# RWKV state stage: k^T V moved into TensorE's first wait, and fewer products of unused result around it

## The reference, cut to what matters

```python
def step(state, inp):
    rt, wt, kt, vt, kkt, at = inp
    sa = jnp.einsum('bhvk,bhk->bhv', state, -kkt)
    state = (state * wt[:, :, None, :]
             + sa[..., :, None] * (kkt * at)[..., None, :]
             + vt[..., :, None] * kt[..., None, :])
    yt = jnp.einsum('bhvk,bhk->bhv', state, rt)
    return state, yt
...
_, y = lax.scan(step, s0, xs)
```

## Time and profile before

| what | value |
|---|---|
| median of 3 runs | 4917.19 us (4914.18 to 4917.27) |
| profiled execution, its own time | 4909.85 us |
| its span | 4908.1 us |
| granted PE clock over the span | 0.947 of full speed |
| stage `rwkv`, PE's first to last product | about 1844 to 2551 us of the span |
| PE busy in the span | 4321.2 us (88%) |
| DVE busy in the span | 2583.5 us (53%) |

### The profile page before, as it was taken

One profiled execution on the slowest core, in us unless ns is written; L12 is line 12 of the kernel. 1 busy time (PEld: TensorE's weight loads), 2 busy tenths in 40 slices (PEclk: granted clock), 3 DMA queues, 4 the chain that ended last, 5 costly groups with the idle time before them and its releaser, 6 DMA issues. The chain is left out here.

```text
span 4908.1 us, 68587 instructions
## 1 busy us (share of the span) xinstructions
PE 4321.2 (88%) x25175; PEld 3600.6 (73%) x25232; DVE 2583.5 (53%) x5011; ACT 1320.3 (27%) x2626; POOL 598.3 (12%) x585
## 2 busy tenths in 40 slices
PE   8999688888599968999978996999989799799879
PEld 6777577777477757888867885778767677577657
DVE  4444434433466656777753334778733433577733
ACT  3223211111222211111112113666621211222211
POOL 0000011111100002333330110000000011011100
PEclk9999799999799988999988998999989899899989
DMA  3111311111433331111113234310033422422233
GB/s 134 48 60 60 126 49 56 63 58 50 151 131 131 131 118 48 36 45 45 45 39 135 109 116 145 104 35 18 10 129 116 155 103 88 154 87 91 75 130 117
DMA packets 218307, 434.14 MB, mean 88 GB/s; under 512 B 36419, under 2 KB 90436, under 8 KB 218022
## 3 DMA queue, kind: packets, MB, share of 16 engines
q1 hardware_dynamic: 218150, 432.08, 25.7%
HBM read 248.40 MB, written 146.93 MB: 81 GB/s over the span
## 5 line engine op out<-in xcount | busy, mean ns | idle before, releaser
L235 PE MATMUL rp_pj<-rp_w_high,rp_hT_high 128*128 128x512 f32 (+1 forms) x640 | 239.3, 383 | 27.2 <-DVE rp_w_low L178 14.4
L235 PE MATMUL fp_pj<-fp_w_high,fp_hT_high 128*128 128x512 f32 (+2 forms) x640 | 220.7, 359 | 46.1 <-DVE fp_w_low L178 46.1
L2515 DVE TENSOR_SCALAR_CACHE_REDUCE fa_sm<-fa_sc 128x512 f32<-128x512 f32 (+2 forms) x320 | 194.4, 610 | 91.9 <-PE fa_sc L2356 80.4
L236 PE MATMUL rp_pj<-rp_w_low,rp_hT_high 128*128 128x512 f32 (+1 forms) x640 | 233.5, 374 | 0.0
L235 PE MATMUL hg_pj<-hg_w_high,hg_hT_high 128*128 128x512 f32 x512 | 210.4, 411 | 16.1 <-DVE hg_w_low L178 16.1
L235 PE MATMUL rc_pj<-rc_w_high,rc_hT_high 128*128 128x512 f32 (+1 forms) x512 | 191.8, 382 | 36.2 <-DVE rc_w_low L178 36.0
L236 PE MATMUL fp_pj<-fp_w_low,fp_hT_high 128*128 128x512 f32 (+2 forms) x640 | 219.1, 357 | 0.0
L236 PE MATMUL hg_pj<-hg_w_low,hg_hT_high 128*128 128x512 f32 x512 | 205.6, 402 | 0.0
L2370 PE MATMUL fa_tp<-fa_ident,fa_sm 128*128 128x128 f32 x1088 | 176.0, 283 | 30.5 <-DVE fa_pT_low L178 14.8
L2463 ACT CAST fa_pT_high<-fa_tp 128x512 fp32r<-128x512 f32 (+1 forms) x288 | 160.9, 559 | 148.9 <-PE fa_tp L2370 146.7
L178 DVE TENSOR_TENSOR fa_pT_low<-fa_tp,fa_pT_high 128x512 fp32r<-128x512 f32 (+1 forms) x288 | 189.0, 657 | 14.7 <-ACT fa_pT_high L2463 14.4
(11 more groups left out here) (557 smaller groups left out, 11225.0 us busy)
## 6 DMA issues: line engine op xcount, KB each, us to landing
rw_given<-rw_packed_dram SPq DMA_DIRECT2D x48, 512.0 KB, 4.1
rc_back<-rc_XB SPq DMA_DIRECT2D x48, 336.0 KB
rw_packed_dram<-rp_M SPq DMA_DIRECT2D x48, 256.0 KB, 2.6
rp_M<-rp_U SPq DMA_DIRECT2D x16, 728.0 KB, 4.8
hg_xt<-in_x SPq DMA_DIRECT2D x16, 512.0 KB, 3.8
kept_x_high_dram<-hg_hT_high SPq DMA_DIRECT2D x16, 512.0 KB, 3.5
kept_x_low_dram<-hg_hT_low SPq DMA_DIRECT2D x16, 512.0 KB, 4.3
sw_hT_high<-kept_x_high_dram SPq DMA_DIRECT2D x16, 512.0 KB, 3.6
```

The costliest lines, as they stand in the source:

```text
L235: pe.matmul(out, hT.high[:, kc, :], self.high[:, kc, lo:hi], start=kc == 0, stop=False)
L236: pe.matmul(out, hT.high[:, kc, :], self.low[:, kc, lo:hi], start=False, stop=False)
L2515: dve.tensor_scalar(sm[:, to:to + cols], bank_of(slot)[:, 0:cols], 0.0, NEG, ALU.add, ALU.max, accum_out=tops[:, four, c:c + 1]).then_inc( ...
```

## The change

Three things are done in `rwkv`, and the banks are dealt out anew so that they fit.

- k^T V becomes a function `pair_up` and runs behind the third group of `multiply`. It is no longer in `read_out`. It writes b6.
- The products of unused result become a function `keep_busy`: six instead of eight in the first place (b7), six instead of twelve in the second (b5).
- `spread` is cut in three: rows 0 to 3 (b7), then after two `masked` rows 4 to 11 (b0, b1), then the fourth `multiply` (b2, b3, after four `masked` instead of two), then after six `masked` rows 12 to 15 (b4). Z is now in b5, Y in b3, and Y's half of `solve` waits for eight `masked`.
- The waits that guard banks move with them: `turn_two` waits for `inc_taken` before it writes b6, the second half of `level` for `y_ready` before it writes b3. The wait for V's load goes from `solve` to `pair_up`.

```diff
--- before.py
+++ after.py
@@ -1424,9 +1424,9 @@
         S = sb("S", [P, PAIRS, P])
         out = [sb(f"out{p}", [P, RW]) for p in range(2)]
         B = [s.bank(f"b{n}") for n in range(8)]
-        Z_BANK, Y_BANK, INC_BANK = 4, 5, 1
+        Z_BANK, Y_BANK, INC_BANK = 5, 3, 6
         TURNED = (("kk", 4), ("r", 5), ("b", 6), ("k", 7))
-        SPREAD = (6, 7, 2, 3)
+        SPREAD = (7, 0, 1, 4)
         spread_row = lambda n: heads(B[SPREAD[n // 4]][:, (n % 4) * P:(n % 4 + 1) * P], RW_HEADS)
 
         CONSTS = 11
@@ -1440,7 +1440,7 @@
         S_in, Z_done, Z_ready, SA_done, SA_ready, y_done, y_ready, inc_done, inc_taken = (sem(n) for n in (
             "S_in", "Z_done", "Z_ready", "SA_done", "SA_ready", "y_done", "y_ready", "inc_done", "inc_taken"))
         var_ready, rstd_ready, out_ready, rest_ready = (sem(n) for n in ("var_ready", "rstd_ready", "out_ready", "rest_ready"))
-        PRODUCT_BANKS = (((0, 1), (2, 3)), ((4, 5), (0, 1)))
+        PRODUCT_BANKS = (((0, 1), (2, 3)), ((4, 5), (2, 3)))
         PER_TILE = 2 * (LEVELS - FIRST)
 
         block = s.block()
@@ -1501,7 +1501,8 @@
                 pe.wait_ge((kr_here, bk_here)[two][pn], 16 * (hn + 1))
                 if two == 0 and t is not None:
                     pe.wait_ge(SA_ready, t + 1)
-                    pe.wait_ge(y_ready, t + 1)
+                if two == 1 and t is not None:
+                    pe.wait_ge(inc_taken, t + 1)
                 for name, bank in TURNED[2 * two:2 * two + 2]:
                     for p in range(PAIRS):
                         last = pe.transpose(B[bank][:, p * P:(p + 1) * P], given_of(pn, name)[:, p * P:(p + 1) * P], ident[:])
@@ -1521,15 +1522,19 @@
                         last = pe.matmul(B[banks[o]][:, cols], lhs[part, p, :], krT[pi][part, p, :, :].rearrange("k n t -> k (n t)"), start=True, stop=True)
                 last.then_inc(products, 1)
 
-            def spread(i, half):
+            def spread(i, a, b):
 
                 pe.wait_ge(parts_ready, i + 1)
-                for n in range(half * SMALL // 2, (half + 1) * SMALL // 2):
+                for n in range(4 * a, 4 * b):
                     bank = B[SPREAD[n // 4]][:, (n % 4) * P:(n % 4 + 1) * P]
                     pe.matmul(bank, pick_row[:, n, :], Up.high[:].rearrange("p h t -> p (h t)"), start=True, stop=False)
                     last = pe.matmul(bank, pick_row[:, n, :], Up.low[:].rearrange("p h t -> p (h t)"), start=False, stop=True)
                     if n % 4 == 3:
                         last.then_inc(spread_done, 1)
+
+            def keep_busy(bank, count):
+                for n in range(count):
+                    pe.matmul(B[bank][:], pick_row[:, n, :], pick_row[:, 4:8, :].rearrange("p n t -> p (n t)"), start=True, stop=True)
 
             def turn_first(i, pi, g):
                 if g == 0:
@@ -1553,8 +1558,8 @@
                     last.then_inc(T1_done, 1)
                 else:
                     pe.wait_ge(T1_ready, done + g + 1)
-                    if l == FIRST and g == 0 and t is not None:
-                        pe.wait_ge(inc_taken, t + 1)
+                    if l == FIRST and g == 1 and t is not None:
+                        pe.wait_ge(y_ready, t + 1)
                     if l > FIRST:
                         pe.wait_ge(XT_ready, done + g - 1)
                     if not top:
@@ -1565,11 +1570,12 @@
                         last = pe.matmul(B[2 * g + 1][0:rows_, 4 * HALF + (h % 4) * HALF:4 * HALF + (h % 4 + 1) * HALF], lhs, halves_of(XT[pi][:, h, :], l, 1), start=True, stop=True)
                     last.then_inc(corr_done, 1)
 
-            def solve(t, pt):
+            def solve(t, pt, i):
                 V = given_of(pt, "v")
                 pe.wait_ge(S_in, t + 1)
-                pe.wait_ge(vg_here[pt], 48)
                 for n, bank in ((0, Z_BANK), (1, Y_BANK)):
+                    if n == 1 and i is not None:
+                        pe.wait_ge(masked, 8 * i + 8)
                     for p in range(PAIRS):
                         pe.matmul(B[bank][:, p * P:(p + 1) * P], krT[pt][:, p, n, :], S[:, p, :], start=n == 0 or p == 0, stop=False)
                         for o in range(2):
@@ -1578,13 +1584,13 @@
                     if n == 0:
                         last.then_inc(Z_done, 1)
 
-            def read_out(t, pt, i):
-                V = given_of(pt, "v")
-                if i is not None:
-                    pe.wait_ge(masked, 8 * i + 8)
+            def pair_up(t, ht, pt):
+                pe.wait_ge(vg_here[pt], 48 * (ht + 1))
                 for p in range(PAIRS):
                     cols = slice(p * P, (p + 1) * P)
-                    pe.matmul(B[INC_BANK][:, cols], given_of(pt, "k")[:, cols], V[:, cols], start=p == 0, stop=False)
+                    pe.matmul(B[INC_BANK][:, cols], given_of(pt, "k")[:, cols], given_of(pt, "v")[:, cols], start=p == 0, stop=False)
+
+            def read_out(t, pt):
                 pe.wait_ge(XT_ready, PER_TILE * (t + 1))
                 pe.wait_ge(Z_ready, t + 1)
                 for h in range(RW_HEADS):
@@ -1611,23 +1617,26 @@
                     multiply(i, pi, 0, 0)
                     multiply(i, pi, 0, 1)
                     multiply(i, pi, 1, 0)
-                    for n in range(8 if m else 0):
-                        pe.matmul(B[SPREAD[0]][:], pick_row[:, n, :], pick_row[:, 4:8, :].rearrange("p n t -> p (n t)"), start=True, stop=True)
-                    spread(i, 0)
+                if m:
+                    pair_up(t, ht, pt)
+                    if pr:
+                        keep_busy(SPREAD[0], 6)
+                if pr:
+                    spread(i, 0, 1)
                     pe.wait_ge(masked, 8 * i + 2)
+                    spread(i, 1, 3)
+                    pe.wait_ge(masked, 8 * i + 4)
                     multiply(i, pi, 1, 1)
-                    pe.wait_ge(masked, 8 * i + 4)
-                    spread(i, 1)
-                if m:
-                    if pr:
-                        pe.wait_ge(masked, 8 * i + 6)
-                    solve(t, pt)
-                    read_out(t, pt, i)
+                    pe.wait_ge(masked, 8 * i + 6)
+                    spread(i, 3, 4)
+                if m:
+                    solve(t, pt, i)
+                    read_out(t, pt)
                 if pr:
                     if not m:
                         pe.wait_ge(masked, 8)
-                    for n in range(12 if m else 0):
-                        pe.matmul(B[0][:], pick_row[:, n, :], pick_row[:, 4:8, :].rearrange("p n t -> p (n t)"), start=True, stop=True)
+                    if m:
+                        keep_busy(Z_BANK, 6)
                     for g in range(2):
                         turn_first(i, pi, g)
                     for l in range(FIRST, LEVELS):
```

## The result

The changed kernel took 4940.46 us (median of 9 runs, 4924.85 to 4947.89), the kernel before 4916.46, run beside it. The ratio is 1.0047, 95% interval 1.0037 to 1.0057: slower by 24 us, where 19 us less was forecast. It is the case of the first rival.

What follows compares the result with a forecast made beforehand. PE's chain was taken as the bound, each step late by PE's own fills. 15 x 1.42 = 21.3 us gained, less 2 for clock falls, gave 4917.19 - 19.3 = 4898 us, range 4887 to 4919.

Steps and rivals of the forecast that it cites:

- first rival: Clock falls in `spread` and stays low: about 10 us per step, two steps eat the gain; chance 0.12 for three or more.
- Twelve fills end 1.6 us behind XT: Ahead of the first transposes, PE's twelve products of unused result last 1.6 us longer than the wait they fill.
- Gain per step at full clock, 1.42: With six fills the first transposes start earlier: 1.42 us saved per step, 21.3 us over 15 steps.
- k^T V at no cost in the first wait, `spread` recut, DVE late by 0.07: k^T V fits PE's wait for DVE's low part, cover 0.1 to 0.2 us; later fourth `multiply` delays DVE 0.07.
- The short falls, +2: Clock falls around the read-out: one in all 15 steps at 1.1 us each, 16.5 against 14.4 now, taken as +2.
- the slack of 0.5: PE's spare time ahead of the first transposes, expected to absorb 0.5 us of each fall's 1.61, leaving 1.1.
- The long falls: Half clock from the end of `spread` toward the fills; no term in the sum, only rival cases, 12 us more at most.
- that 16 such products with an idle ahead never lowered the clock in 15 full steps: Argument from the old trace's `spread` products against a clock fall there, where the change has 24; that case got chance 0.12.
- The transposes at half clock, or DVE late by 0.5: At PE's new waits: transposes cost 1.03 us more per step (chance 0.02), or DVE is late by 0.5 (0.08).
- third rival: Gain half eaten at PE's new waits, by late `multiply` or slow transposes: 4907 to 4913 us; chance 0.10.
- DVE's wait ahead of its first join: DVE's wait before joining the first level was to shrink from 2.17 to about 0.75 us, leaving DVE free in time.

Runs made afterwards that it cites:

- b_fill6: The kernel before the change with six instead of twelve products of unused result ahead of the first transposes, nothing else; 4886.01 us, ratio 0.9935 to before.
- a_recut: The changed kernel with the fourth `multiply` put back behind 16 `spread` products instead of 24; 4901.89 us, ratio 0.9971 to the kernel before.
- a_fill8: The changed kernel with eight products of unused result in the first wait instead of six; 4900.02 us, ratio 0.9966 to the kernel before.
- a_fill5: The changed kernel with five products of unused result in the first wait instead of six; 4937.14 us, ratio 1.0039 to the kernel before.
- a_late: The changed kernel with k^T V back between `solve` and the read-out and eight products of unused result in the first wait; 4964.74 us, ratio 1.0092.
- b_sa: The kernel before with two products of unused result added in SA's wait and four instead of twelve ahead of the first transposes; 4879.74 us, ratio 0.9919.

## Why the prediction was wrong, point by point

- *Twelve fills end 1.6 us behind XT.* Right. b_fill6 takes six away and nothing else: steps of 40.85 instead of 42.24.
- *Gain per step at full clock, 1.42.* Right, 1.49 measured (42.24 - 40.75): 14 x 1.49 = 20.9 us in the 14 steps.
- *k^T V at no cost in the first wait, `spread` recut, DVE late by 0.07.* Right at full clock (0.17 of cover, the masks late by 0.10, XT not late at all). k^T V's place gave back nothing, as the sum had it.
- *The short falls, +2.* Near by luck. 630.97 - 14 x 40.75 - 45.55 for the long ones leaves 14.92 us, against 605.81 - 14 x 42.24 = 14.45 before: +0.47. But the sum had a fall in each of 15 steps at 1.1 us. Eight of the 14 steps have one, as before, at 1.9 each (14.9 / 8): the slack of 0.5 takes nothing off, and the two errors cancel.
- *The long falls.* Here it failed. The step that failed is the one that put them at nothing: the sum had no term for them, and they cost 10.56 + 12.17 + 10.56 + 12.26 = 45.55 us over the 40.75 of an undisturbed step. -20.86 + 0.47 + 45.55 = +25.16, which is 630.97 - 605.81. The first rival had the place and the turning point (two steps) right and the price nearly (10 each). Two of the four cost more than its upper end (12 less 0.5): the clock stays down 27 us in them, into the transposes, whose eight records take 1.43 us. (With four such steps it made 4938; 4940 came.) Its chance of 0.12 was what was wrong, and with it which case was the likeliest.
- *The argument that gave that chance* was "that 16 such products with an idle ahead never lowered the clock in 15 full steps". But the change has 24 of them and an idle amid them, and `multiply`, which ended the old stretch after 1.94 us, now comes after 3.27 (1988.02 to 1991.29). a_recut puts it back behind 16 and the long falls are gone; a_fill8 shortens the stretch from the other side and they are gone too. Evidence for a shorter stretch was taken for the longer one.
- *The transposes at half clock, or DVE late by 0.5* (third rival). Neither came: in every step without a fall, with four to six fills ahead of them, the eight records of the first transposes take 1.03 to 1.10 us, against 1.03 before. (Its lower end is 4906 by its own sum, 4917.19 - 15 x 0.9 + 2, not 4907.)

The median moved by 24.0 us and the 14 steps by 25.2. The span moved by 30.6. The other 5.4 are a start of the stage 4.9 later and a first step 4.4 longer, less 3.9 in what follows the 14 steps. The start varies in all these kernels (1847.7 to 1858.6 us), and I don't put these parts down to the change.

What stays open: why some steps with the thin stretch have a long fall and others, whose rows read alike, don't, and why one fill less (a_fill5) brought fewer of them in its profile and no more time. The experiments show that the stretch is needed, not what picks the step. Two things in the traces narrow it. All fifteen long falls in these profiles begin 8.4 to 8.7 us into their step, as the stretch ends. And in a_late their order repeats: from the fourth step on, the steps take 51, 41, 51, 51, 41 us and then the same five again. So the choice isn't mere scatter. It may hang on when in a step the clock can change, which the lengths of the steps before it shift; that is an inference, and no run here was built to test it.

## What to carry to other kernels

Filling a wait with products costs nothing only while the fill ends before the wait does: compare the end of the fill with the end of what is waited for, and cut the rest. A change that leaves PE as busy as before can still lower its clock, if it lines up short products that stood apart; so look for the longest row of them after the edit, not only at idle time. A few 512-column products cost nothing where PE waits anyway: here two in a wait of 0.68 us and four instead of twelve behind were worth 36 us (b_sa), and six instead of twelve alone 32 (b_fill6).

## What the runs showed of the hardware

- The granted clock fell to 0.5 with PE busy 7.61 of the 8 us ahead of it. What PE did ahead of every long fall was `spread`, up to 24 float32r products of 128 columns with one idle of 0.2 us among them; ahead of every short one, the 64-column products around SA's wait. The Trainium skill says in "TensorE: Matmul & The Clock Gate", "What's actually happening", that the throttle depends on how busy PE has been and that activity releases it. The trace agrees on the two levels (1.00 and 0.50), but the busy share of the profile doesn't tell which of them comes.
- Once down, the clock stayed down for 17 to 27 us in the long falls, although PE was busy 24.32 of 25.00 us: `solve` and the 64-column products didn't bring it back. It came back behind products of 128 columns in fp32: b^T SA in the step shown (at 2141.5), k^T V in a_late (0.7 us behind them, after 17 us); in the falls of 27 us it came back only in the fills or the first transposes behind b^T SA.
- Two of DVE's operations of 128x512 with both inputs in SBUF took 1.60 instead of 0.69 us where POOL made CT at the same time. In the step at 1982 us (timelines of DVE and POOL):

```profile
2008.87 1.60 DVE L1743 TENSOR_TENSOR rw_y<-rw_y,rw_rstd 128x512 f32<-128x512 f32 x1
2010.55 1.61 DVE L1743 TENSOR_TENSOR rw_out<-rw_y,rw_rest 128x512 f32<-128x512 f32 x1
```

```profile
2008.39 3.21 POOL L1706 TENSOR_TENSOR rw_CT<-rw_BA,rw_blocks 128x512 f32<-128x512 f32 x2 [10.98 <-PE rw_b L1557]
```

  Before, the last of the two had begun when POOL started, and took 0.69:

```profile
2177.34 0.69 DVE L1734 TENSOR_TENSOR rw_out<-rw_y,rw_rest 128x512 f32<-128x512 f32 x1
```

```profile
2177.57 2.82 POOL L1697 TENSOR_TENSOR rw_CT<-rw_BA,rw_blocks 128x512 f32<-128x512 f32 x2 [12.46 <-PE rw_b L1552]
```

  So DVE's wait ahead of its first join went from 2.17 to nothing instead of to 0.75. It cost no time: PE's chain from the first transposes to the next step is 0.06 us longer (2023.26 - 2005.75 = 17.51 against 17.45), but that stands in the transposes themselves, ahead of the join (1.09 us instead of 1.03). The Trainium skill's "GPSIMD Engine Reference", "Specifications", says that GpSimd shares its SBUF interfaces with VectorE and that they contend when VectorE has two SBUF inputs; the trace agrees.
